# Sparse attention fed without the norm's factor, top-k in pieces, stick-breaking's last scores ahead of a value block, another order at the RWKV opening

## The reference

```
x = x + mixer(rms_norm(x, norm_mix[i]));  x = x + swiglu(rms_norm(x, norm_ffn[i]))
rms_norm(x, g) = x * rsqrt(mean(x * x) + 1e-6) * g
```

```
q, k, v, qi, ki, wi = split(h @ w_in)          # qi: 8 index heads of 64, ki: 1
q, k = rope(rms_norm(q)), rope(rms_norm(k));  qi, ki = rope(qi), rope(ki)
score = sum_h wi_h * relu(qi_h . ki);  the 64 keys with the highest score of each query are attended
```

## Time and profile before

| | |
|---|---|
| median of three runs | 1893.09 us |
| the profiled execution's own time | 1889.73 us |
| its span | 1887.8 us |
| mean granted TensorE clock | 0.981 |
| busy: PE, PEld | 1806.7, 1619.7 us |
| busy: DVE, ACT, POOL | 1218.3, 1045.0, 70.9 us |
| loaded from HBM | 284.03 MB, 151 GB/s over the span |

### The profile page before, as it was taken

How to read it: one execution, slowest core, us unless ns; L and a number is a source line. 1 busy time by engine, 2 the same in 40 slices (tenths; PEclk the granted TensorE clock), 3 DMA queues, 4 the chain that set the end, 5 groups by cost and what they waited for, 6 DMA issues and landing times.

```text
span 1887.8 us, 41717 instructions
## 1 busy us (share of the span) xinstructions
PE 1806.7 (96%) x17879; PEld 1619.7 (86%) x17879; DVE 1218.3 (65%) x1783; ACT 1045.0 (55%) x1623; POOL 70.9 (4%) x58
## 2 busy tenths in 40 slices
PE   6999999999989999899999999999999999998998
PEld 5898798899979888797798898898798898897887
DVE  6853577855437775487678856754577756765764
ACT  5855465554436554354665556865465544564554
POOL 0001000000000000114000000001000000000000
PEclk9999999999989999899999999999999999998998
DMA  6330256567657555356475562410255554443441
GB/s 186 127 104 4 69 186 196 179 196 236 205 177 253 190 193 183 111 159 195 141 211 195 180 207 94 135 62 4 82 185 182 193 186 146 137 151 118 137 135 67
DMA packets 288526, 287.75 MB, mean 152 GB/s; under 512 B 15240, under 2 KB 286456, under 8 KB 288344
## 3 DMA queue, kind: packets, MB, share of 16 engines
q1 hardware_dynamic: 285048, 283.98, 47.4%
q10 hardware_dynamic: 3296, 1.11, 0.3%
HBM read 284.03 MB, written 1.05 MB: 151 GB/s over the span
## 4 chain that ended last, share of the span: by engine, by line
PE 90%; DVE 5%; ACT 3%; issue 1%; DMA 0%; SPq 0%; DVEq 0%; POOL 0%; ACTq 0%; POOLq 0%
PE ps L412 23%; PE ps L413 12%; PE ps L389 10%; PE ps L391 9%; PE ps L390 9%; PE ps L815 2%; PE ps L429 2%; PE ps L430 2%; PE ps L431 2%; PE ps L711 1%; PE ps L791 1%; PE ps L725 1%; PE ps L800 1%; PE ps L639 1%; PE ps L824 1%
## 5 line engine op out<-in xcount | busy, mean ns | idle before, releaser
L456 DVE TENSOR_TENSOR wl<-raw,wh 128x1024 fp32r<-128x1024 f32 x484 | 585.8, 1228 | 339.1 <-ACT wh L446 334.2
L446 ACT ACTIVATE wh<-raw 128x1024 fp32r<-128x1024 f32 x484 | 499.7, 1042 | 445.4 <-PE ps L413 190.6
L412 PE MATMUL ps<-HH,wh 128*128 128x512 f32 x1408 | 489.8, 391 | 0.0
L413 PE MATMUL ps<-HH,wl 128*128 128x256 f32 x1408 | 397.0, 282 | 0.0
L412 PEld LDWEIGHTS ps<-HH,wh 128*128 128x128 f32 x1408 | 264.3, 188 | 55.6 <-issue 0.4
L389 PE MATMUL ps<-HH,wh 128*128 128x256 f32 x928 | 270.2, 291 | 11.3 <-DVE HH L2558 6.2
L413 PEld LDWEIGHTS ps<-HH,wl 128*128 128x128 f32 x1408 | 266.1, 189 | 0.1
L390 PE MATMUL ps<-HH,wh 128*128 128x256 f32 x928 | 262.3, 283 | 0.0
L391 PE MATMUL ps<-HH,wl 128*128 128x256 f32 x928 | 261.9, 282 | 0.0
L389 PEld LDWEIGHTS ps<-HH,wh 128*128 128x128 f32 x928 | 177.8, 192 | 20.7 <-issue 5.5
L390 PEld LDWEIGHTS ps<-HH,wh 128*128 128x128 f32 x928 | 178.0, 192 | 1.2 <-issue 1.2
(11 more groups left out here) (323 smaller groups left out, 3001.2 us busy)
## 6 DMA issues: line engine op xcount, KB each, us to landing
raw<-in_ffn_w_gu_dram SPq DMA_DIRECT2D x88, 1024.0 KB, 5.1
raw<-in_ffn_w_down_dram SPq DMA_DIRECT2D x32, 1024.0 KB, 5.3
raw<-in_w_in_dram SPq DMA_DIRECT2D x32, 1024.0 KB, 5.7
raw<-in_rw_w_rkv_dram SPq DMA_DIRECT2D x24, 1024.0 KB, 5.4
B<-in_w_ada_dram SPq DMA_DIRECT2D x24, 1024.0 KB, 8.2
raw<-in_ds_w_in_dram SPq DMA_DIRECT2D x14, 1024.0 KB, 5.3
raw<-in_ffn_w_down_dram SPq DMA_DIRECT2D x16, 768.0 KB, 4.4
raw<-in_sb_w_qkv_dram SPq DMA_DIRECT2D x12, 1024.0 KB, 5.7
```

Of the source, the lines that this page charges most:

```text
L412: e.matmul(o[:, m, :], h_[:, k, c], x_, start=k0 + k == 0, stop=False, skip_group_check=True)
L413: i = e.matmul(o[:, m, 0:S], l_[:, k, c], x_[:, 0, :], start=False, stop=k0 + k == kt - 1, skip_group_check=True)
L446: e.activation(wh[:, u % UNITS, 0:kn * 256], raw[:, j % RAW, k0 * 256:(k0 + kn) * 256], ACT.Copy).then_inc(*up("hi"))
L456: e.tensor_tensor(wl[:, u % UNITS, 0:kn * 256], raw[:, j % RAW, k0 * 256:(k0 + kn) * 256], wh[:, u % UNITS, 0:kn * 256].bitcast(F32), ALU. ...
```

## The change

Sparse attention: the FFN of layer 1 now gets `gain`, so HH and HL hold x times the norm's weights when the mixer begins. `pe_dsa` has no barrier any more and runs the first block of qi before the norm's sum. ScalarE makes x times the weights in float32 for ki. The factor rstd is applied at the exits: VectorE multiplies qi, ki, q and k by it as it copies them out of PSUM (ScalarE did the copies before), and v and wi by rstd turned by two transposes. The top-k rounds are spread: four and four for the first keys, 1, 2, 2, 2 and 1 for the second, between the exits, splits and ropes.

Stick-breaking: `scores(3)` stands ahead of `block("v", 3)`, and sums, values, modulation steps, roundings and rests of the end are in another order. The `w_ada` pieces 8 to 11 go to other buffers, two of them when the last scores have been taken, two after the last value block, with six semaphores in place of four.

RWKV: in layer 0 the first two parts of the low-rank weights are combined before rstd is there. ScalarE prepares the second mix later, and its sigmoids and conversions come earlier. VectorE runs the splits and running sums before the second mix. The four key norms follow two blocks of r. The tail is computed as one product with both weight parts side by side (`gt`), copied to `lor`, and combined with a shift by two matmuls with the identity (`gv`), after the third block of r. The products with the decay are made before the key norm's factor is there (`decayed`), and the third mix is prepared after them.

```diff
 # pe_rwkv
-            for g in range(3):
+            full(0, 1, 0)
+            full(0, 1, 1)
+            for g in range(4):
                 key_norm(g)
-            full(0, 1, 0)
-            key_norm(3)
-            full(0, 1, 1)
-            pe_lora(e, ("gv", n), tail, tail_mixed, 0, 64 if n else 32, h, ("dve", ("lora tail", n)))
+            tw = 32 + 32 * n
+            o = bank(e, ("gt", n), ("act", ("gt", n)))
+            e.wait_ge(*at("dve", ("lora tail", n)))
+            for k in range(KD):
+                i = e.matmul(o[0:2 * tw, 0:S], tail[:, k, 0:2 * tw], h[:, k, :], start=k == 0, stop=k == KD - 1, skip_group_check=True)
             full(0, 1, 2)
+            o = bank(e, ("gv", n), ("act", ("gv", n)))
+            e.wait_ge(*at("act", ("gt", n)))
+            e.matmul(o[0:tw, 0:S], ident[0:2 * tw, 0:tw], lor[0:2 * tw, :], start=True, stop=False, skip_group_check=True)
+            e.matmul(o[0:tw, 1:S], ident[0:2 * tw, tw:2 * tw], lor[0:2 * tw, 0:S - 1], start=False, stop=True,
 # act_rwkv (after the key norms)
+            e.activation(lor[0:2 * tw, :], PS("gt", n)[0:2 * tw, 0:S], ACT.Copy).then_inc(*up("act", ("gt", n)))
             hi(e)
             evac(0, 1, R_)
             clear(0)
             clear(1)
+            hi(e)
+            evac(0, 2, R_)
             e.wait_ge(*at("mm", ("gv", n)))
             e.activation(sg[0:32, 1, :], PS("gv", n)[0:32, 0:S], ACT.Sigmoid).then_inc(*up("act", ("gv", n)))
-            hi(e)
-            evac(0, 2, R_)
+            for g in range(4):
+                rounded(2, HH, g, ("unit", ("full", n, 1, 3)))
 # dve_rwkv
+            if n == 0:
+                dve_lora(e, 0, 3, 4)
             e.wait_ge(*at("act", (("rms w", n), "rstd")))
 ...
+            erase_and_write(0)
+            erase_and_write(1)
+            lo(e)
             prepare(2, (HH, HL), ("unit", ("full", n, 1, 3)), ("dve", ("k2", n, 3)))
-            erase_and_write(0)
-            lo(e)
-            erase_and_write(1)
-            lo(e)
 # pe_stickbreak
+            scores(3)
             block("v", 3)
             values(2)
-            scores(3)
             pe_mod(e, 2)
             pe_ada(e, 3)
+            sums(3)
             pe_mod(e, 3)
             pe_ada(e, 4)
-            sums(3)
+            values(3)
             pe_mod(e, 4)
             pe_ada(e, 5)
-            values(3)
-            pe_mod(e, 5)
             cur["first"] = 0
             pe_out_proj(e, layer, parts_of(XH, XL), [[("dve", ("ol", layer, k // 2))] for k in range(KD)])
+            pe_mod(e, 5)
 # pe_dsa
-            barrier(e, "mm", ("ds", 0))
-            pe_rms(e, ("rms d", 0), None, ("f", layer - 1))
+            fm_block(e, ("ds", "qi", 0), KD, h, [[("dve", ("xl", "f", layer - 1, k // 2))] for k in range(KD)], ("dve", ("ds", "qi", 0)))
+            pe_rms(e, ("rms d", 0), None, ("f", layer - 1))
+            fm_block(e, ("ds", "qi", 1), KD, h, None, ("dve", ("ds", "qi", 1)))
 # dve_dsa
+            def block(name, g, dst):
+                e.wait_ge(*at("unit", ("ds", name, g)))
+                e.tensor_tensor(dst[:, 2 * g:2 * g + 2, :], two(PS("ds", name, g)[:, :]), rb, ALU.mult).then_inc(*up("dve", ("ds", name, g)))
```

More of the change, by code:

```diff
@@ L1785, in act_stickbreak @@
                 weights(g)
-                hi(e)
+                if g < 2:
+                    hi(e)
+            act_ada(e, 2)
             softened(3)
-            act_ada(e, 2)
+            hi(e)
+            rounded(0)
+            rounded(1)
             act_ada(e, 3)
+            weights(3)
+            rounded(2)
             act_ada(e, 4)
-            weights(3)
-            for g in range(3):
-                if g == 0:
-                    e.wait_ge(*at("mm", ("ada block", 8)))
-                rounded(g)
+            rounded(3)
             act_ada(e, 5)
-            rounded(3)
             act_add_x(e, "o", layer, ("norm_ffn", layer))
@@ L1864, in norm @@
                                  scale=-0.5).then_inc(*up("act", ("ds", "rn " + name, g)))
-            for g in range(2):
-                block("qi", g, qi)
-            e.wait_ge(*at("mm", ("ds", "ki")))
-            o = PS("ds", "ki")
-            e.activation(ki, o[:, 0:S], ACT.Copy).then_inc(*up("act", ("ds", "ki")))
-            e.activation(wi, o[:, S:S + 16].rearrange("p (j e) -> p j e", j=2), ACT.Copy, scale=float(8 ** -0.5 * 64 ** -0.5)).then_inc(*up("act", ("ds", "wi")))
+            hi(e)
+            hi(e)
             block("q", 0, q_, FM(11))
@@ L2279, in dve_rwkv, with running_sums @@
             prepare(1, (HH, HL))
-            prepare(0, (XH, XL), ("dve", ("xml", n, 1, 3)))
+            def running_sums():
+                for k in range(KD):
+                    e.wait_ge(*at("act", ("w2", n, k // 2)))
+                    e.tensor_tensor_scan(cum[:, k, :], C("scan"), cum[:, k, :], 0.0, ALU.mult, ALU.add).then_inc(*up("dve", *([("cum", n)] if k == 7 else [])))
             lo(e, 2 if n else 4)
@@ L2283, in dve_rwkv @@
                 e.wait_ge(s_rest, 16)
-            for k in range(KD):
-                e.wait_ge(*at("act", ("w2", n, k // 2)))
-                e.tensor_tensor_scan(cum[:, k, :], C("scan"), cum[:, k, :], 0.0, ALU.mult, ALU.add).then_inc(*up("dve", *([("cum", n)] if k == 7 else [])))
-            for g in range(3):
-                lo(e)
-                new_key(g)
+            running_sums()
+            lo(e)
+            prepare(0, (XH, XL), ("dve", ("xml", n, 1, 3)))
+            lo(e)
+            new_key(0)
+            lo(e)
             if n == 0:
@@ L2498, in dve_stickbreak @@
             dve_mod(e, 2)
-            soft(3)
+            rest(0)
+            rest(1)
+            rest(2)
             dve_mod(e, 3)
-            dve_mod(e, 4)
-            for g in range(3):
-                rest(g)
             heads_out(3)
             rest(3)
+            dve_mod(e, 4)
+            dve_add_x(e, "o", layer, ("norm_ffn", layer))
             dve_mod(e, 5)
-            dve_add_x(e, "o", layer, ("norm_ffn", layer))
         def dve_softmax_attn(e, L, bias):
@@ L2611, in dve_dsa @@
             e.memset(score, 0.0).then_inc(*up("dve"))
+            block("q", 0, q_)
             lo(e)
```

194 lines of the change are left out of this document (115 added, 79 removed).

## The result

The changed kernel takes 1873.80 us (median of 4 runs, 1873.49 to 1875.27) against 1893.42 us of the kernel before on the same chip: a ratio of 0.9898, 95% interval 0.9884 to 0.9912. The prediction was 1875.4 us. The profiled execution has a span of 1871.5 us, 16.3 less than before.

What follows compares the result with a forecast made beforehand. TensorE, busy 96% of the span, was taken as the bound. RWKV -0.1, stick-breaking -8.8 and sparse attention -8.8 sum to -17.7: 1889.73 to 1872.0 us, plus 3.4 for the median gives 1875.4; range 1860 to 1885.

Steps and rivals of the forecast that it cites:

- Opening of layer 0: RWKV layer 0: TensorE starts at 16.2; second low-rank stage ends at 34.9, not 41.4: -6.5 us.
- The tail and what took its place: RWKV layer 0: TensorE waits 5.5 us at the tail's bank for ScalarE; with 2.2 for clock, -1.4 us in all.
- Rival one: RWKV layers 0 and 3: ScalarE in time, no wait for the tail's bank, -14.0 us, 1861.5 in total; chance 0.17.
- Layer 3: RWKV layer 3: -4.9 us saved, waits of 3.7 and 1.6 added, 0.9 for clock: +1.3 us.
- Stick-breaking: End of stick-breaking: 10.0 us of losses go, 1.4 of new waiting, 0.2 more gained: -8.8 us, bounds -10 and 0.
- rival three: Stick-breaking: weights of the last modulation products take the gain back, +8.8 us, 1884 in total; chance 0.14.
- sign of being wrong: No ScalarE wait at `pb`, q/k blocks waiting for splits, or a modulation product waiting for its DMA.
- Sparse attention, opening: Index heads of sparse attention start at 800.3, not 808.7, with 1.1 us for clock: -8.4 us, bounds -4 and -11.
- The middle: Middle of sparse attention: q/k copies give VectorE 69.2 us against TensorE's 79.4; a 0.7 us wait goes: -0.6 us.
- Rival two: Middle of sparse attention: VectorE becomes the bound, 104 us against 79.4: +25 us, 1900 in total; chance 0.05.
- The table loads: ScalarE chains: the skill's 1.38 us drain would add 5.5 us, 1886 in all; the trace disagreed, so nothing was charged.
- Rival four: Exits at the end of layer 1 cost what sparse attention's opening gives: within 0.2%; chance 0.04.

Runs made afterwards that it cites:

- tail_16: Changed kernel with the low-rank tail as before: 16 matmuls ahead of the first half's block 2, no identity product; 1871.15 us, ratio 0.9891 to the kernel before.
- bank_shift: Changed kernel with the ring of banks taken up one bank later in the RWKV layers; 1877.84 us, ratio 0.9923 to the kernel before.
- rwkv_only: Kernel before with the RWKV part of the change alone; 1891.74 us, ratio 1.000 to the kernel before.
- topk_block: Changed kernel with sparse attention's top-k rounds back in three blocks (8, 4 and 4 rounds); 1880.55 us, ratio 0.9947 to the kernel before.
- dsa_only: Kernel before with the sparse attention part of the change alone; 1884.33 us, ratio 0.996 to the kernel before.
- after_again: The changed kernel again, word for word, in a later set of runs; 1876.26 us, ratio 0.992 to the kernel before.
- exits_first: Changed kernel with the index queries' exits ahead of the split of the pair that waits for weights; 1874.68 us, ratio 0.9915 to the kernel before.

## Why the prediction was right, and where its terms were off

**Opening of layer 0.** Forecast: TensorE starts at 16.2 behind an idle 1.6; it was 16.26 behind 1.69. The second low-rank stage ended at 33.9, 1.0 us sooner than forecast, because the 0.9 us charged for half clock were not lost in this execution. That charge is a mean of two things: in 4 of the 11 profiled executions with this opening, the first products took 1.19 and 1.06 us for two rather than 0.67 and 0.59, and the tail came 2.6 to 3.0 us later; in the 7 others, nothing.

**The tail and what took its place.** Right in place, and nearly in size: ScalarE's event at 86.7 rather than 88.3, a wait of 4.9 rather than 5.5. That the level products came at 98.42, where the working has 98.4 before its charge for clock, is luck: the wait ended 1.5 us sooner than forecast, and half clock then took 1.5 us from `pb` (3.64 us rather than 2.1). With the 2.2 us for clock the forecast for them was 100.6. Layer 0 as a whole gained 1.6 us, forecast 1.4, because 2.0 of the 3.6 us were lost again behind the level products; there the trace has 3.4 us at half clock (from 226.8 on), and none before. The reason was half told. I put the wait down to the tail's bank; `tail_16` and `bank_shift` show that the time comes from what stands on ScalarE and VectorE, and that the bank only names the place. Rival one fell with it: even with no wait at that bank nothing is gained.

**Layer 3.** The step that failed in size. The kept bank's wait was 3.6 (3.7 forecast). The second wait, 1.6 us at `bp`'s eighth bank, wasn't there (`rwkv_only` and `bank_shift` had 0.6 us of it). In its place the clock: 5.1 us lost at the opening and behind it, against 1.7 before, where I charged 0.9. So +2.1, not +1.3. Over all executions: 421.5 to 423.1 us for this layer with the old order (3), 425.2 to 430.9 with the new one and nothing that mends it (7). The changed kernel's first profile is the shortest of these, so +2.1 is the small end of what this layer costs.

**Stick-breaking.** -7.5 and -7.7 in two profiles, not -8.8. The wait behind the last value block is 1.5 (1.4 forecast); what is missing, 1.1 to 1.3, is about the wait for the last `w_ada` pieces (1.4 and 1.3), which stood in the bounds and not in the sum. It is the small end of rival three, and one of the things that the prediction named as a sign of being wrong.

**Sparse attention, opening.** -9.7 in the changed kernel's first profile, -8.4 forecast. The chain was right almost step by step. The forecast counts from a first block at 767.9; it started 9.0 us sooner, at 758.9, by what the layers before had gained. Less 9.0, its marks are 775.6 for the weights, 784.1 for ki and 790.2 for GpSimd's last rope; measured were 775.5, 783.6 and 789.8, and the index scores began at 789.98. ScalarE's wait for the weights:

```profile
775.52 2.00 ACT L446 ACTIVATE wh<-raw 128x1024 fp32r<-128x1024 f32 x2 [8.15 <-DMA raw<-in_ds_w_in_dram]
```

The term that was off is the 1.1 us for clock: the half clock fell on the rotations (3.51 us for four, 1.95 in the second profile), behind which TensorE had to wait for ki anyway, so it idled 1.1 us rather than 2.7 and lost nothing. In the second profile the index scores come 2.5 us later (792.46), and only part of that is clock. VectorE's pair of splits in front of ki, with GpSimd's first rope, first in the changed kernel's first profile, then in the second, with TensorE's wait behind it:

```profile
780.67 2.36 DVE L456 TENSOR_TENSOR wl<-raw,wh 128x1024 fp32r<-128x1024 f32 x2
782.23 1.93 POOL L2897 TENSOR_TENSOR B<-B 128x512 f32<-128x512 f32 x1 [31.97 <-PE ps L1219]
...
780.49 3.42 DVE L456 TENSOR_TENSOR wl<-raw,wh 128x1024 fp32r<-128x1024 f32 x2
781.10 1.74 POOL L2897 TENSOR_TENSOR B<-B 128x512 f32<-128x512 f32 x1 [30.82 <-PE ps L1219]
784.66 1.19 PE L1219 MATMUL ps<-B,CT 128*128 128x256 f32 x2 [2.88 <-DVE B L2660]
```

The rotation at full clock let GpSimd start 1.1 us sooner, inside the pair; the pair took 1.1 us longer, ki came 0.9 us later, and the block behind it ran partly at half clock, 1.3 us longer. In the eight executions with this opening and the old order of exits the gain is 5.6 to 9.7 us, so the margin is not a safe one.

**The middle.** -0.9, forecast -0.6, with VectorE at 69.5 us (69.2 forecast). Rival two fell: 25.6 us of GpSimd beside it did no harm in this stretch. A split beside GpSimd's ropes took longer here too (3.4 us for the pair at 825.26), as "SBUF — State Buffer" of the Trainium skill has it ("SBUF: two separate sides") and the earlier trace rows show. That TensorE waits for none of them goes with the pieces in which the rounds come, and `topk_block` puts 4.5 us on those; what part GpSimd has in these 4.5 us isn't shown.

**The table loads.** Here too the sigmoid begins at the end of its 1.28 us load, so that the drain of 1.38 us that "ScalarE: Activation LUTs" of the Trainium skill gives ("What ACT_TABLE_LOAD costs") was rightly left out.

Rival four fell with `dsa_only`. Its price was wrong too: without the opening's 8.4 us the forecast still has 9.3 us of gain, which is 0.5% and not within 0.2%. One reading at the start said too much as well: that the clock is below full in four of forty slices only. A 9 in that row is anything from 90% up, and the trace has twelve stretches at half clock, 71 us in all.

The total is right within 1.6 us, and part of that is luck. From profile to profile, with the forecast in brackets: layer 0 -1.6 (-1.4), layer 3 +2.1 (+1.3), stick-breaking -7.5 (-8.8), sparse attention -10.6 (-8.8), the rest +1.2 (0), in all -16.4 (-17.7). The errors have both signs. And the medians lie 19.6 us apart, not 16.3, because the median lay 3.7 us above the profiled execution before (3.4 with the three runs of the prediction) and 0.3 us above it in the changed kernel.

## What to carry to other kernels

When work is taken from the engine that bounds the kernel, ask what the next common product needs from all engines: if that chain stays, the time only changes into a wait, and moving a PSUM bank moves the wait. Shorten the chain instead (here one weight pair moved behind two roundings, 2 us a layer). Where the bounding engine waits anyway, products that nobody reads cost little here and went with a higher clock; they are worth a try, with the clock of every run beside the time. A profile of one execution shows a chain well and a gain of 3 us badly: before such a difference is believed, the same kernel should be run again.

## What the runs showed of the hardware that I had not expected

- Executions of one kernel lie up to 21 us apart, and where profiles could be compared it was mostly the clock that differed. In kernels that differ in a few lines elsewhere, the same attention took 42.6, 43.5 and 50.0 us, behind idle pieces of 1.9 and 2.4 to 2.9 us each time. Behind the same two pieces (1.93 and 2.88) half clock lasted 3.4 us in `after_again` and 20.5 us in `exits_first`, so the idle pieces alone don't decide how long it lasts.
- Half clock at the very start isn't in the granted clock of the windows. In the four executions with first products of 1.19 rather than 0.67 us, the trace has no clock record until 22.1 to 22.3 us, and the windows print 1.00 for want of one; in the seven others the records begin at 12.2 to 15.2 us.
- Half clock at the rotations of sparse attention: 3.4 us from 779.7 on in the changed kernel, with 0.86 us of idle time there; 6.8 us from 780.0 on in `exits_first`, with no idle time ahead of it. What causes it is open.
- The releaser named at a wait on several events was ScalarE in `tail_16` and `bank_shift`, while the event that came last was VectorE's.
- GpSimd's start decides what a VectorE split costs: the same pair took 2.36 us when the rope began 1.6 us after it, and 3.42 us when it began 0.6 us after it. A faster clock on TensorE brought the rope forward, and the index scores came later.
